# A two-block sequence model on one core: four column groups of the gate projection move into the delta stage, whose tiles share places, and the merge weights are fetched behind them

## What is computed

```python
h = _rmsnorm(x, w['norm_w']) * (1.0 + scale[:, None]) + shift[:, None]
na_q, na_k, na_v, na_z, dn_qkv, dn_z, dn_b, dn_a, g_na, g_dn = _split_proj(h @ w['w_in'])
...
o_na = _na_latent(q, k, v, kc, vc, w['na_rpb'])          # neighbourhood attention
...
def step(S, xs):                                          # gated delta rule, chunks of 64 tokens
    qk_i, qd_i, kd_i, u_i, w_i, gt_i = xs
    v_new = u_i - jnp.einsum('bhck,bhkv->bhcv', w_i, S)
    o_i = jnp.einsum('bhck,bhkv->bhcv', qd_i, S) + jnp.einsum('bhij,bhjv->bhiv', qk_i, v_new)
    S = S * gt_i[..., None, None] + jnp.einsum('bhck,bhcv->bhkv', kd_i, v_new)
    return S, o_i
...
u_na = (o_na.reshape(B, T, NA_WIDTH) * jax.nn.silu(z_na)) @ w['w_o_na']
u_dn = (o_dn * jax.nn.silu(z_dn)) @ w['w_o_dn']
y = jax.nn.sigmoid(g_na) * u_na + jax.nn.sigmoid(g_dn) * u_dn
return y @ w['w_out']
```

## Time and profile before

| what | value |
|---|---|
| median of three runs | 3821.64 us |
| lowest and highest run | 3807.43 and 3835.5 us |
| span of the profiled execution | 3830.8 us |
| PE busy in it | 3185.6 us (83%) |
| DVE, ACT, POOL busy | 2138.3, 1316.2, 572.5 us |
| HBM read and written | 257.46 and 118.94 MB |

### The profile page before, as it was taken

One profiled execution on the slowest core, in us unless ns is written; L12 is line 12 of the kernel. 1 busy time (PEld: TensorE's weight loads), 2 busy tenths in 40 slices (PEclk: granted clock), 3 DMA queues, 4 the chain that ended last, 5 costly groups with the idle time before them and its releaser, 6 DMA issues. The chain is left out here.

```text
span 3830.8 us, 82729 instructions
## 1 busy us (share of the span) xinstructions
PE 3185.6 (83%) x36140; PEld 2617.9 (68%) x36140; DVE 2138.3 (56%) x3567; ACT 1316.2 (34%) x2374; POOL 572.5 (15%) x466
## 2 busy tenths in 40 slices
PE   7999986656999999645479998779899789886699
PEld 7988874543498888534335897778788578786344
DVE  3445538886625555479775365466665355453452
ACT  3133325642321333355433132234444122121441
POOL 0200004431002000145210021001110122121100
PEclk9999997767999999855589999899999599898799
DMA  4522213224326221131253344453331321111430
GB/s 132 168 95 78 78 44 93 76 71 152 135 95 195 80 78 47 55 72 48 89 172 109 140 149 145 164 185 118 111 113 43 112 48 48 37 40 58 154 107 33
DMA packets 270500, 379.79 MB, mean 99 GB/s; under 512 B 46389, under 2 KB 209517, under 8 KB 268792
## 3 DMA queue, kind: packets, MB, share of 16 engines
q1 hardware_dynamic: 168074, 261.54, 22.1%
q10 hardware_dynamic: 102066, 112.97, 8.5%
HBM read 257.46 MB, written 118.94 MB: 98 GB/s over the span
## 5 line engine op out<-in xcount | busy, mean ns | idle before, releaser
L385 PE MATMUL psum<-proj_w_low,h_high 128*128 128x344 f32 (+1 forms) x1984 | 668.6, 337 | 16.9 <-DVE proj_y L411 13.4
L385 PE MATMUL psum<-proj_w_high,h_high 128*128 128x344 f32 (+1 forms) x1984 | 657.6, 331 | 0.0
L385 PE MATMUL psum<-proj_w_high,h_low 128*128 128x344 f32 (+1 forms) x1984 | 656.6, 331 | 0.0
L385 PEld LDWEIGHTS psum<-proj_w_low,h_high 128*128 128x128 f32 x1984 | 376.2, 190 | 33.6 <-DVE proj_y L411 15.6
L385 PEld LDWEIGHTS psum<-proj_w_high,h_high 128*128 128x128 f32 x1984 | 376.0, 190 | 6.8
L385 PEld LDWEIGHTS psum<-proj_w_high,h_low 128*128 128x128 f32 x1984 | 375.8, 189 | 7.1
L385 PE MATMUL psum<-proj_rest_w_low,h_high 128*128 128x304 f32 x640 | 207.0, 323 | 33.7 <-DVE proj_rest_w_low L400 21.9
L1424 PE MATMUL psum<-w_out,merge_yt 128*128 128x512 f32 x512 | 226.5, 602 | 1.8 <-DVE merge_yt L1307 1.8
L868 POOL TENSOR_TENSOR scan_d<-scan_b 128x384 f32<-128x384 f32 x112 | 123.7, 1105 | 625.0 <-DVE scan_b L709 612.2
L411 DVE COPY proj_y<-psum 128x344 f32<-128x344 f32 (+1 forms) x130 | 70.4, 541 | 245.7 <-PE psum L385 236.9
L1168 DVE COPY diff_wt<-psum 128x512 f32<-128x512 f32 x64 | 44.3, 692 | 282.2 <-PE psum L1114 282.2
(11 more groups left out here) (411 smaller groups left out, 6727.8 us busy)
## 6 DMA issues: line engine op xcount, KB each, us to landing
proj_raw<-in_w_in SPq DMA_DIRECT2D x24, 1376.0 KB, 6.9
proj<-proj_y ACTq DMA_DIRECT2D x192, 172.0 KB, 1.9
delta_x<-dn_qkv SPq DMA_DIRECT2D x40, 384.0 KB, 5.2
...
```

What stands on the lines that cost most here:

```text
L385: last = PE.matmul(self.ps[:, j % self.banks, 0:self.width], hp[:, kt, tokens], wp[:, c % 2, kt, :], start=kt == 0 and n == 0, stop=kt == ...
```

## The change

The `z` and `g` columns are cut anew. `proj2_rest` keeps 7 groups of 288 columns (56 items), at 1, 2.43, 3.86, ... The last 1024 columns (the gates) become a second `Project`, `proj2_last`: 4 groups of 256 columns, 32 items, each written out in four pieces of 6 matmuls, with the results in PSUM banks 6 and 7. It runs in the delta stage from virtual time 8, an item every 3.1, a piece every 0.775.

To make room, `Delta` lets tiles share places (`gm` is `dec`, `kbg` is `kb`, `o` is `lt`, `um` and `vn` are `xt`, `wt` is `xm`; one `tk`, one `ct`, one set of `ym`; x has two buffers instead of three), with the waits that this asks for, and its state part uses the chunk's own banks. Bank c mod 3 is thus free for chunk c+3 only when `o_added(c)` is done, where it was `u_copied(c)`. The steps' times are set anew (0 becomes 1.1, 18 to 20.75 become 17.9 to 19). The clearing of `ym` falls from 15 tiles to 5.

The weights of the merge (`w_branches` and `w_out_2`, 8 MB) are fetched by SP in the delta stage at virtual time 112, behind the last product of `proj2_last`, and ACT's load in `Merge2` is gone.

```diff
 class Project
-                if self.halves and kt == KT // 2:
-                    yield j + 0.5
+                if kt and kt % (KT // self.pieces) == 0:
+                    yield j + kt / KT
...
 class Fetch
     def sp(self):
         yield 0
+        if self.after is not None:
+            self.nc.sync.wait_ge(*self.after.product(self.after.items - 1))
...
 class Delta, pe_chunk
-        yield 0
-        PE.wait_ge(*self.loaded[s](2 * (c // Z) + 1))
+        yield 1.1
+        PE.wait_ge(*self.loaded[c % 2](2 * (c // 2) + 1))
         if c >= Z:
-            PE.wait_ge(*self.u_copied(c - Z))
+            PE.wait_ge(*self.o_added(c - Z))
...
-        yield 1
+        yield 1.5
...
-        yield 2
+        yield 2.2
...
-        A, sm, wt = 2 * Z, self.sm, self.wt[s]
-        yield 18
+        sm, wt = self.sm, self.wt[s]
+        yield 17.9
+        PE.wait_ge(*self.u_copied(c))
         if c:
             PE.wait_ge(*self.state(c - 1))
-            PE.wait_ge(*self.o_added(c - 1))
...
-        yield 19
+        yield 18.4
...
-        yield 20
+        yield 18.8
 class Delta, dve_chunk
-        yield 0.75
+        yield 1.2
         V.wait_ge(*self.placed(c))
+        if c >= Z:
+            V.wait_ge(*self.w_made(c - Z))
         V.tensor_tensor(h3(self.kb[s][:]), h3(k_), per(beta), ALU.mult).then_inc(*self.weighted.inc())
...
-        yield 18.5
+        yield 18.1
...
-        yield 19.5
+        yield 18.6
...
-        yield 20.5
+        yield 18.95
 class Delta, act_chunk
-        yield 0.25
+        yield 1.3
         S.wait_ge(*self.mirrored(c))
...
-        yield 20.75
+        yield 19
         S.wait_ge(*self.o_added(c))
 class Merge2, act
-        S.dma_start(self.wo[:], self.a["w_out_2"].rearrange("a (k p) n -> p (a k) n", p=P)).then_inc(*self.weight.inc())
 def build
-        rest = Project(k, "proj2_rest", above, h, [late] * 10, w2, 304, p2, 3136, row2, 2, ctx=h_ctx, banks=2, halves=True)
+        rest = Project(k, "proj2_rest", above, h, [late] * 7, w2, 288, p2, NZ + 32, row2, 2, ctx=h_ctx, banks=2, pieces=2)
...
-        together(k, (rest, 1, 1.0), (gates, 4, 1.5), (na, 1, 0.6), (prepare, 20, 1.1), (attention, 23, 0.9))
-        delta = Delta(k, dn, dg, o_dn)
+        together(k, (rest, 1, 1.43), (gates, 4, 1.5), (na, 1, 0.6), (prepare, 20, 1.1), (attention, 23, 0.9))
+        last = Project(k, "proj2_last", above, h, [late] * 4, w2, 256, p2, NZ + 32 + 7 * 288, row2, 2, ctx=h_ctx, banks=2, pieces=4, out=(6, 7))
+        delta = Delta(k, dn, dg, o_dn, last.top)
...
-        together(k, (delta, 0, 1.0), (Fetch(k, "w_branches", [(wb[:, 0:4], kp("w_o_na_2")), (wb[:, 4:8], kp("w_o_dn_2"))]), 0, 1.0))
-        run(k, Merge2(k, p2, mod, o_na, o_dn, xs, wb))
+        weights = Fetch(k, "merge2_weights", [(wb[:, 0:4], kp("w_o_na_2")), (wb[:, 4:8], kp("w_o_dn_2")), (wo[:], kp("w_out_2"))], last)
+        together(k, (delta, 0, 1.0), (last, 8, 3.1), (weights, 112, 1.0))
+        run(k, Merge2(k, p2, mod, o_na, o_dn, xs, wo, wb, above))
```

124 lines of the change are left out of this document (67 added, 57 removed).

## The result

| | before | after |
|---|---|---|
| median of four runs | 3828.32 us | 3915.55 us |
| lowest and highest run | 3807.43 and 3835.5 | 3906.77 and 3925.74 |
| span of the profiled execution | 3830.8 | 3918.3 |

The ratio is 1.0242, with a 95% interval of 1.0213 to 1.0271. The change makes the kernel 87 us slower. The forecast was 3819 with a range up to 3872, so the prediction is wrong.

The account below looks back on a forecast made before the run. The prediction took PE (TensorE) to bound both the rest and delta stages. Rest stage -68, delta stage +74 and merge start -9 summed to -3 us: 3819 us on the median, range 3768 to 3872.

Parts of the forecast that it names:

- in both stages TensorE's order is what ends last: Rest and delta stages: PE, 89% busy, bounds both, so work moved from one to the other is not removed.
- Price of the moved work: Moved projection: 0.119 us per matmul of 256 columns plus 0.25 us turnover a piece; 0.96 us a piece, 123 us for 128.
- I take 1.6 of the 2.25 us: Attention turns: of 2.25 us less PE work a turn, 1.6 shortens it, 53 us in all (bounds 30 and 74).
- what a turn needs without any projection ... 8.8 us: Attention: the turn's own steps, such as scores, bias, maximum, exponential, transposes and handovers, take 8.8 us together.
- the attention's loop holds the rest stage at -35: Rest stage: a case where the attention's loop limits the gain to 35 us (3852), counted within the 0.45 chance of no change.
- Work, 27.5 forecast: Delta stage: a period with pieces, no waits and a full clock takes 27.5 us, 20.1 of present work plus 7.4 of pieces.
- Waits, 2.4 forecast: Delta stage: new waits of 2.4 us a period, for `grown`, `inner`, gate sums and DVE updates; today's waits are covered.
- Clock, 1.5 us of loss forecast to end: Delta stage: 14% of the time passes at 1.2 GHz; if that ends, 1.5 us a period of work go.
- So they cost nothing there: Delta stage: the 8 MB of merge weights take 23 us of the 110 left, at a DMA share of 0.08, for free.
- Start, -12 forecast: Delta stage start: fewer `ym` tiles to clear and a higher clock give -12 us (bounds 0 and -25).
- the holes are filled: Rival, rest and delta stages: rest stage gains 90 us, pieces hide all delta waits, period 27.9; 3761 us, chance 0.30.
- the state chain: Rival, delta stage: the pressed state chain becomes the bound, waits 6.0 instead of 2.4 us a period; 3881 us, chance 0.25.

Follow-up runs that it names:

- tenth experiment: The changed kernel with a chunk's first steps spread out to later times (gate sums at 2.1, scores at 4.3), pieces and three sets kept: 3894.57 us, ratio 1.0152.
- experiment 13: The changed kernel with the late half of the delta rule's preparation as its own stage behind the rest stage: attention turn 11.35 us in one run.
- four sets: Four sets of tiles and banks instead of three, against the new layout and order with all ten column groups in the rest stage: 3900.14 us, ratio 1.0192.
- the twelve kernels above: The study's twelve kernels that fetch the 8 MB in the delta stage and start a chunk every 6 units; their 16th period takes 32.1 to 41.4 us.
- fourth experiment: The changed kernel with the rest stage's items dense again (pace 1.0), so the attention's later turns have no piece: 3920.11 us in one run.

## Why the prediction was wrong, step by step

**What bounds the kernel.** The step "in both stages TensorE's order is what ends last" held for the delta stage. It failed for the attention as soon as work was taken away. PE's 89% there was read as PE being the bound with 11% open, but the attention's own chain over DVE and ACT stood close behind it: 2.0 us less of PE's work a turn made the turn 0.3 us shorter, and 0.1 behind the first turn.

**Price of the moved work: right, a little high.** PE's matmuls of 256 columns follow each other after (3146.74 - 3146.27) / 4 = 0.118 us, where 0.119 was forecast; the first takes 0.22:

```profile
3146.05 0.38 PE L390 MATMUL psum<-proj_last_w_low,h_high 128*128 128x256 f32 x1
3146.27 0.28 PE L390 MATMUL psum<-proj_last_w_high,h_high 128*128 128x256 f32 x1
...
3146.74 0.28 PE L390 MATMUL psum<-proj_last_w_high,h_low 128*128 128x256 f32 x1
```

Of the 128 pieces 118 lie in the 19 periods (708 matmuls), and they hold 101 us more work than before, 0.86 a piece; by the tenth experiment's row, with hardly any half clock in it, 113 us and 0.95. The forecast had 0.96. The rule for the gap between matmuls gave 0.109 for 256 columns (the Trainium skill, TensorE: Matmul & The Clock Gate, Back-to-back issue gap, which gives it as the gap of an isolated matmul); the trace does not agree, and the row was the better guide.

**Rest stage, -68 forecast, -17.5 measured.** The failed step is "I take 1.6 of the 2.25 us". PE's work fell by 2.0 us a turn, near the 2.25. The turn fell by (393 - 384) / 31 = 0.3. Its other half, "what a turn needs without any projection ... 8.8 us", had summed the attention's own steps. It left out the work for the delta rule's preparation, which stands between them in the orders of DVE and ACT (0.8 to 1.0 us a turn, experiment 13), and whatever else keeps a turn without preparation at 11.3. The waits view of after shows where the freed time stands, for 2546:2930. It is the attention's own chain, scores behind the bias, transposes behind the exponential:

```profile
PE psum L1762 <- DVE na_sc L1826: 21.9, 18, 4.0
PE psum L1781 <- ACT na_sc L1883: 13.7, 8, 5.1
PE psum L1795 <- ACT na_sc L1883: 13.3, 14, 4.8
PE psum L1781 <- DVE na_ot L1836: 12.5, 9, 3.0
```

In the same stretch before, the first of these is 5.8 us and the second 6.3. The text named this case ("the attention's loop holds the rest stage at -35", "380 the loop") and made it too mild: from the first scores to the delta stage 405 us pass, where 417 stood and 360 or 380 were named. It also put the case inside "within 1%", although it then needed all other terms to go well. The 15 us taken ahead of the attention were 5.9 (bounds 5 and 28). And of the 9 us gained in the 31 turns 7 came from the first, which the reading of 31 like turns had hidden; so even the -17.5 owe little to the mechanism that was forecast.

**Delta stage, +74 forecast, +117 measured.** With pieces the period was forecast at 29.9 and is 31.5. The 30.3 above is a mean over 19 and hides that.
- *Work, 27.5 forecast.* Over the 15 periods with pieces it is 413 us, 27.5 a period, by two errors that cancel. The 24.3 us of today's period counted the two short ones at the end; ahead of them a period is 25.3, with 20.7 of work where 20.1 were taken. The pieces were 0.5 us a period cheaper than forecast. That the number is met is luck.
- *Waits, 2.4 forecast.* They are 35 us in the 15 periods, 2.4 each. But the sum had the waits of today covered and new ones in their place. The new ones were named and sized nearly right. In the layout without pieces the gate sums wait 1.1 (0.8 forecast), the state 0.8 (0.5), `vn` and `o` 0.4 (0.5). But they come on top of the old ones there, 5.6 us idle in all, and the pieces then fill half of it: 2.8 after over the 19. "A step has 4 us of other chunks' work ahead of it, now 1.2 us more" is right as far as this goes. The larger part sits where I gave 0.8 and 0.4: the mirroring now stands directly ahead of the gate sums. With four sets and no pieces, putting these first steps apart gives 3.05 us a period; the state part, to which I gave the rival's title, gives no more than 0.5. With three sets and the pieces, setting them apart to the later side gave 1.2 (30.3 to 29.1).
- *Clock, 1.5 us of loss forecast to end.* It didn't. Over the 15 periods with pieces the granted clock is 0.95, not "0.98 or more in the steady part", and the loss 1.6 us a period for 1.8 before. That is the whole of 31.5 less 29.9. Over all 19 the clock even fell, 0.93 to 0.92, with 0.80 in the last four (0.96 before). The rival's reading that the 92 us at 0.59 hold "up to as much" as 25 us is also off: 0.41 x 92 is 38.
- *The last four periods and the fetch.* I let the pieces lengthen 14.8 periods and the others be as before. The first 15 became 91 us longer (83 forecast), the last four 23 (none forecast), 114 in all. Of the 23, 18 lie in the one period in which the 8 MB move. "So they cost nothing there" is a term put at nothing because the DMA share was low; in the twelve kernels above that period is 5 to 11 us over its neighbours. In the change these 10 us are as much as the merge start gives.
- *Start, -12 forecast, -1.7 measured* (79.3 to 77.6). Two windows rows, of before and of after, show why. The clock did rise, 0.53 to 0.67, and gave back what the 10 pieces of the start (60 matmuls) cost, no more.

```profile
2972.00:3051.00 79.00, 56.59 (x787) 42.19 (x791) 28.65 (x62) 10.60 (x27) 13.82 (x12) 0.53 0.40 116
```

```profile
2951.00:3029.00 78.00, 54.49 (x896) 40.72 (x900) 27.81 (x54) 15.70 (x32) 14.43 (x13) 0.67 0.34 84
```

- *End, +3 forecast.* It was meant for the three periods without pieces, and those are in the 23 us above. Behind the last `faded` come another 4.3 (19.0 to 23.3), so the end as a whole was wrong.

**Merge start, -9 forecast, -9.4 measured: right**, by its own steps, though the fetch that makes it possible seems to take as much in the delta stage. `merge_e` starts 9.4 us behind the stage's first transfer (8.5 forecast for the landing of tile 0), and DVE's first instruction 17.4 us behind it (17 forecast, 27 before):

```profile
3628.28 0.34 SPq L2630 DMA_DIRECT2D merge_o<-o_dn  x1
...
3637.63 2.76 ACT L2689 ACTIVATE merge_e<-merge_z 128x3072 f32<-128x3072 f32 x1 [20.80 <-DMA merge_o<-o_na]
...
3645.65 0.69 DVE L2757 TENSOR_REDUCE merge_ss<-merge_ob 128x8 f32<-128x512 f32 x1 [20.64 <-DMA merge_mg<-modulation]
```

**The rivals.** The first, "the holes are filled", describes half of what happened: the pieces did fill the holes, but those that the change had opened itself. The second had the right sign and called its mechanism "the state chain". Its premise that chunk c+3 can't be mirrored before `o_added(c)` is true and, by the four sets, does not cost by itself; what costs there is that the mirroring stands against the gate sums. Both rivals let the rest stage gain at least 68 us. A rival with the attention's loop and the layout together, which is what came, was not priced.

**What stays open.** Why the granted clock is 0.92 in the changed kernel and 0.98 with the first steps set apart, with equal idle time in the window (54 and 53 us), is not settled; the same delta stage at 0.96 in the fourth experiment says that a part of it is not the edit. Nor is it shown what holds a turn of the attention at 11.3 us. That the pressed first steps are what costs is shown with four sets and without pieces; in the changed kernel, with three sets, a cost of holding the banks until `o_added` is not excluded. No run takes away the fetch of the 8 MB alone.
